# Late phase boundaries: the residual turned by plain transposes and scaled afterwards, with ScalarE's and VectorE's orders, and four one-column products for sixteen

## What is computed

```python
def second_block(...):
    for l in range(DEPTH):
        h = rmsnorm(x, norm_pre[l, 0]) * (1.0 + sc1) + sh1
        y = swiglu(h, ffn_w_gate[l, 0], ffn_w_up[l, 0], ffn_w_down[l, 0])
        x = x + 0.5 * g1 * rmsnorm(y, norm_post[l, 0])
        h = rmsnorm(x, norm_pre[l, 1]) * (1.0 + sc2) + sh2
        y = hybrid_mixer(h, ...)
        x = x + g2 * rmsnorm(y, norm_post[l, 1])
        ...
```

## Time and profile before

| | before |
|---|---|
| median of 3 runs | 3181.19 us (3179.10 to 3194.51) |
| the profiled execution | 3182.83 us |
| its span | 3181.0 us |
| mean granted clock of TensorE | 0.989 |
| busy: PE, DVE, ACT, POOL | 3090.9, 2255.9, 1637.7, 692.7 us |
| chain that ended last | PE 86%, DVE 8%, DMA 2%, ACT 2% |

### The profile page before, as it was taken

The page is one execution under the profiler, slowest core; times in us unless marked ns, Lnnn a source line. Parts: engine busy times, 40 slices in busy tenths (PEclk is TensorE's granted clock), DMA queues, the critical chain, the costliest instruction groups (busy, mean ns, idle before and its releaser), DMA issues.

```text
span 3181.0 us, 58397 instructions
## 1 busy us (share of the span) xinstructions
PE 3090.9 (97%) x19928; PEld 2753.1 (87%) x19928; DVE 2255.9 (71%) x4134; ACT 1637.7 (51%) x3094; POOL 692.7 (22%) x692
## 2 busy tenths in 40 slices
PE   6999999999999999999999999999999999999999
PEld 5779999988888876899999788879987998988898
DVE  6649988877777435798888677777666777766654
ACT  1225578864444354355888444455455545445543
POOL 0107845520000110285555000000100010010000
PEclk9999999999999998999999999999999999999999
DMA  7635555558887431455444788877854787884354
GB/s 284 240 134 167 187 165 173 163 204 264 262 259 253 130 120 40 136 184 170 139 138 133 251 263 262 261 248 260 264 197 141 248 262 257 276 260 144 123 183 152
DMA packets 178000, 635.86 MB, mean 200 GB/s; under 512 B 23976, under 2 KB 23984, under 8 KB 177232
## 3 DMA queue, kind: packets, MB, share of 16 engines
q1 hardware_dynamic: 134560, 491.48, 46.9%
q0 software_dynamic: 43296, 142.77, 13.5%
q10 hardware_dynamic: 16, 0.01, 0.0%
HBM read 630.88 MB, written 9.53 MB: 201 GB/s over the span
## 4 chain that ended last, share of the span: by engine, by line
PE 86%; DVE 8%; DMA 2%; DVEq 2%; ACT 2%; issue 1%; SPq 0%; ACTq 0%
PE ps L773 21%; PE ps L597 12%; PE ps L599 11%; PE ps L598 11%; PE ps L755 7%; PE ps L585 6%; PE ps L632 2%; PE ps L1167 2%; PE ps L1166 2%; PE ps L1035 1%; DMA ring<-stream 1%; PE ps L968 1%; PE ps L873 1%; PE ps L701 1%; PE ps L660 1%
## 5 line engine op out<-in xcount | busy, mean ns | idle before, releaser
L1781 DVE TENSOR_TENSOR unit_low<-ring,unit_high 128x1024 fp32r<-128x1024 f32 x480 | 638.8, 1331 | 172.3 <-ACT unit_high L1267 163.8
L1267 ACT CAST unit_high<-ring 128x1024 fp32r<-128x1024 f32 x524 | 548.2, 1047 | 230.6 <-PE ps L599 167.3
L599 PE MATMUL ps<-expert_x_high,unit_low 128*128 128x256 f32 x1968 | 556.1, 283 | 0.0
L597 PE MATMUL ps<-expert_x_high,unit_high 128*128 128x256 f32 x1552 | 447.9, 289 | 2.0 <-DVE unit_low L1781 1.8
L598 PE MATMUL ps<-expert_x_low,unit_high 128*128 128x256 f32 x1552 | 433.8, 280 | 0.0
L599 PEld LDWEIGHTS ps<-expert_x_high,unit_low 128*128 128x128 f32 x1968 | 370.5, 188 | 0.0
L773 PE MATMUL ps<-unit_low,expert_high 128*128 128x512 f32 x1016 | 325.1, 401 | 2.4 <-DVE unit_low L1781 2.4
L773 PE MATMUL ps<-unit_high,expert_high 128*128 128x512 f32 x1016 | 317.6, 393 | 4.6 <-ACT unit_high L1267 4.4
L773 PE MATMUL ps<-unit_high,expert_low 128*128 128x512 f32 x1016 | 320.1, 395 | 0.1
L597 PEld LDWEIGHTS ps<-expert_x_high,unit_high 128*128 128x128 f32 x1552 | 294.2, 190 | 6.5 <-issue 2.6
L598 PEld LDWEIGHTS ps<-expert_x_low,unit_high 128*128 128x128 f32 x1552 | 293.3, 189 | 0.0
(11 more groups left out here) (388 smaller groups left out, 7054.6 us busy)
## 6 DMA issues: line engine op xcount, KB each, us to landing
ring<-stream SPq DMA_DIRECT2D x754, 512.0 KB, 4.1
arena<-stream SPq DMA_DIRECT2D x160, 512.0 KB, 4.3
score<-ada POOLq DMA_DIRECT2D x128, 512.0 KB, 5.1
arena<-ada POOLq DMA_DIRECT2D x96, 512.0 KB, 5.1
arena<-bias_tiles POOLq DMA_DIRECT2D x48, 192.0 KB, 2.7
arena<-ada SPq DMA_DIRECT2D x8, 1024.0 KB, 17.3
bias_tiles<-bias_rows POOLq DMA_DIRECT2D x8, 768.0 KB, 14.9
arena<-gate_home POOLq DMA_DIRECT2D x7, 512.0 KB, 10.3
```

Source lines behind the costliest of these rows:

```text
L597: pe.matmul(out, hi[:, kt, :], xh[:, kt, :], start=(kt == 0), stop=False)
L599: mm = pe.matmul(out, lo[:, kt, :], xh[:, kt, :], start=False, stop=(kt == KD - 1))
L1267: nc.scalar.copy(hi, raw_of(unit)).then_inc(whi_ready, 1)
L1781: V.tensor_tensor(out=lo, in0=raw_of(unit), in1=hi, op=ALU.subtract).then_inc(wlo_ready, 1)
```

## The change

1. `turn_x` transposes x with the plain identity as its pieces arrive, so that it needs no root. After 6 dummies, two products spread the inverse roots of the two token halves over all partitions, into banks 3 and 2 (`row_scaled`).
2. DVE copies these rows to SBUF, multiplies each turned tile by its gain and by the row (`turned_in`), and ACT adds the shift (`shift`, as in the earlier phases). For a feed-forward phase DVE makes the low half from the unshifted tile in one instruction per tile.
3. ACT squares the first token half of x in one instruction of 1024 columns, after the last root of y. DVE does all four adds, then the inverses; the third unit's subtraction moves behind the adds, ahead of the second inverse.
4. In the hybrid POOL adds the squares of a group's four chunks, so that four one-column products do for sixteen; in round 3 DVE subtracts the unit `b + 3` ahead of the copies of the outputs.
5. Dummies: 14 for 12 at the hybrid's end, 6 for 8 at peer1's, none at the last phase's.

```diff
-            def turn_x(no, bank):
+            def turn_x(ph, bank):
+                i = PHASES.index(ph)
                 for tt in range(TT):
-                    pe.wait_ge(x_scaled, TT * no + tt + 1)
                     for kt in range(KD):
-                        mm = pe.matmul(hx(kt)[:, tt * P:(tt + 1) * P], xt[:, tt, kt * P:(kt + 1) * P], stat[:, tt, 0:P],
-                                       start=True, stop=True)
-                        if tt and kt % 2:
-                            mm.then_inc(hx_ready, 1)
-                    if tt == 0:
-                        busy(3, bank)
+                        if kt % 4 == 0:
+                            pe.wait_ge(x_ready, KD * (i - 1) + (4, 6, 6, 8)[2 * tt + kt // 4])
...
+                        pe.transpose(hx(kt)[:, tt * P:(tt + 1) * P], xt[:, tt, kt * P:(kt + 1) * P], ident)
+                busy(6, bank)
+                for tt in range(TT):
+                    pe.wait_ge(x_scaled, TT * (i - 4) + tt + 1)
+                    pe.matmul(ps[3 - tt][:, 0:P], x_inv[:, tt:tt + 1].to_broadcast([P, P]), ident,
+                              start=True, stop=True).then_inc(row_scaled, 1)
...
-                pe.wait_ge(osq_ready, KD * (l + 1))
+                pe.wait_ge(osq_added, 6 * (l + 1))
                 for grp in range(2):
                     for tt in range(TT):
-                        for kt in range(4):
-                            mm = pe.matmul(ps[3][:, 2 * grp + tt:2 * grp + tt + 1], sq[:, 4 * grp + kt, tt * P:(tt + 1) * P],
-                                           ones[:, 0:1], start=(kt == 0), stop=(kt == 3))
+                        mm = pe.matmul(ps[3][:, 2 * grp + tt:2 * grp + tt + 1], sq[:, 4 * grp, tt * P:(tt + 1) * P],
+                                       ones[:, 0:1], start=True, stop=True)
...
+            def x_first_half(ph):
+                act.wait_ge(x_ready, KD * PHASES.index(ph) + 4)
+                nc.scalar.activation(junk[:, 0:2, :], xt[:, 0, :].rearrange("p (q n) -> p q n", q=2), ACT.Square,
+                                     accum_out=x_sum[:, 0:1])
                 act.drain()
+                nc.scalar.activation(x_root[:, 0:1], x_sum[:, 0:1], ACT.Sqrt, bias=eps, scale=1.0 / D).then_inc(x_rooted, 1)
...
             def turned_in(ph):
                 vec = vec_of(ph)
-                for q in range(4):
-                    dve.wait_ge(h_ready, KD * norm_no_h[ph] + 2 * q + 2)
-                    for kt in (2 * q, 2 * q + 1):
-                        V.tensor_scalar(hT[:, kt, :], hx(kt), acol[:, kt:kt + 1], mods[:, vec, kt:kt + 1], ALU.mult, ALU.add)
-                    dve.drain()
-                    V.tensor_tensor(out=xparts[:, 1, 2 * q:2 * q + 2, :], in0=hT[:, 2 * q:2 * q + 2, :],
-                                    in1=xparts[:, 0, 2 * q:2 * q + 2, :], op=ALU.subtract).then_inc(xlo_ready, 2)
+                for tt in range(TT):
+                    dve.wait_ge(row_scaled, TT * (PHASES.index(ph) - 4) + tt + 1)
+                    V.tensor_copy(stat[:, 0, tt * P:(tt + 1) * P], ps[3 - tt][:, 0:P])
+                dve.drain()
+                for kt in range(KD):
+                    V.scalar_tensor_tensor(out=hT[:, kt, :], in0=hx(kt), scalar=acol[:, kt:kt + 1], in1=stat[:, 0, :],
+                                           op0=ALU.mult, op1=ALU.mult).then_inc(mid_ready, 1)
+                for kt in range(KD if ph.startswith("ffn") else 0):
+                    dve.wait_ge(h_ready, KD * norm_no_h[ph] + kt + 1)
+                    V.scalar_tensor_tensor(out=xparts[:, 1, kt, :], in0=hT[:, kt, :], scalar=mods[:, vec, kt:kt + 1],
+                                           in1=xparts[:, 0, kt, :], op0=ALU.add, op1=ALU.subtract).then_inc(xlo_ready, 1)
...
                 y_scale(1)
                 add(2)
+                add(3)
                 if more:
                     x_scaled_of(ph, 0)
-                add(3)
-                if more:
-                    x_halved_of(ph, 1)
+                    x_halved_of(ph)
+                    if nxt:
+                        low(start[nxt] + 2, split0[nxt] + 2)
                     x_scaled_of(ph, 1)
...
+                def add_squares(r):
+                    pool.wait_ge(osq_ready, KD * l + r + 1)
+                    first, chunk = 4 * (r % 2), r // 2 + 4 * (r % 2)
+                    pool.drain()
+                    G.tensor_tensor(out=sq[:, first, :], in0=sq[:, first, :], in1=sq[:, chunk, :], op=ALU.add).then_inc(osq_added, 1)
```

More of the change, by code:

```diff
@@ L1083, in hyb @@
                 pe.wait_ge(first_mixed, l + 1)
-                busy(12, ps[0])
+                busy(14, ps[0])
             def ffn(ph, no, u):
@@ L1216, in peer @@
                     pe.wait_ge(xt_ready, 1)
-                    busy(8)
+                    busy(6, ps[1])
                     return
@@ L1290, in shift @@
                     act.wait_ge(mid_ready, KD * n + kt + 1)
-                    nc.scalar.activation(hT[:, kt, :], hT[:, kt, :], ACT.Identity, bias=mods[:, vec, kt:kt + 1]).then_inc(h_ready, 1)
-            def turned_in(ph):
-                no = PHASES.index(ph) - 4
-                for kt in range(KD):
-                    act.wait_ge(hx_ready, 4 * no + kt // 2 + 1)
                     out = xparts[:, 0, kt, :] if ph.startswith("ffn") else hT[:, kt, :]
-                    nc.scalar.activation(out, hx(kt), ACT.Identity, bias=mods[:, vec_of(ph), kt:kt + 1],
-                                         scale=acol[:, kt:kt + 1]).then_inc(h_ready, 1)
-                if ph.startswith("ffn"):
-                    have(ACT.Silu)
+                    nc.scalar.activation(out, hT[:, kt, :], ACT.Identity, bias=mods[:, vec, kt:kt + 1]).then_inc(h_ready, 1)
             def x_square(ph, k):
@@ L1738, in peer @@
                     x_square(ph, 3)
[L1739 removed]
+                    x_second_half(ph)
                     return
@@ L1749, in _ @@
             for ph in phases:
-                if late_phase(ph):
-                    turned_in(ph)
-                else:
+                if not late_phase(ph):
                     norm_in(norm_no[ph], ph)
-                    if ph == "mix0":
-                        act.wait_ge(ada_read, 2)
-                    shift(ph, vec_of(ph))
+                if ph == "mix0":
+                    act.wait_ge(ada_read, 2)
+                shift(ph, vec_of(ph))
+                if ph.startswith("ffn"):
+                    have(ACT.Silu)
                 u = start[ph]
@@ L1871, in add @@
                     V.tensor_tensor(out=piece_of(xt, k), in0=piece_of(xt, k), in1=piece_of(yt, k), op=ALU.add).then_inc(x_ready, 2)
-                for k in range(3):
+                for k in range(4):
                     gated(k)
                     add(k)
-                x_halved_of(ph, 0)
-                gated(3)
                 x_scaled_of(ph, 0)
-                add(3)
-                x_halved_of(ph, 1)
+                x_halved_of(ph)
+                low(start[nxt] + 2, split0[nxt] + 2)
                 x_scaled_of(ph, 1)
-                low(start[nxt] + 2, split0[nxt] + 2)
             def add_normed(ph):
@@ L1949, in add_normed @@
                     gate(0)
-                    if nxt:
-                        low(start[nxt] + 2, split0[nxt] + 2)
                     gate(1)
@@ L2286, in hyb @@
                         project(qs[:, 0], ps[1], b3[:, i + 1, :], -SCALE)
+                    if i == 3:
+                        low(b + 3, m + 3)
                     take_outputs(r, i)
@@ L2291, in hyb @@
                         lowest(g, k, causal[k])
-                    low(b + 4 if i < 3 else b + 3, m + 3)
+                    if i < 3:
+                        low(b + 4, m + 3)
                     for k in range(2):
@@ L2686, in hyb @@
                             bias(e, f, i + (16 + 4 * f) if e == 0 else i * 2 + (24 + f))
+                    for r in (2 * i - 2, 2 * i - 1) if i >= 2 else ():
+                        add_squares(r)
+                add_squares(6)
+                add_squares(7)
             def row_out(ph, col):
```

40 lines of the change are left out of this document (18 added, 22 removed).

## The result

| | before | after |
|---|---|---|
| median, first comparison | 3180.14 us (4 runs) | 3158.71 us (4 runs, 3155.66 to 3166.69) |
| ratio | | 0.9923, 95% interval 0.9897 to 0.9948 |
| median, later runs | 3180.25 to 3185.48 us | 3161.75 us (12 runs), 0.9933 (0.9911 to 0.9955) |
| profiled execution, its span | 3182.83, 3181.0 us | 3166.69, 3164.9 us |
| chain that ended last | PE 86%, DVE 8% | PE 90%, DVE 4% |

What follows compares the result with a forecast made beforehand. PE, busy for 97% of the span, was taken as the bound. Hybrids 11.7 plus handoffs 5.5 gave 17.2 us: 3182.8 to 3165.6 us for a profiled execution, 3164 us for the median, range 3154 to 3175.

Steps and rivals of the forecast that it cites:

- one-column products: Tail of both hybrids on PE: going from 16 products to 4 saves 2.6 and about 2.8 us, 5.4 us.
- half clock behind them: PE behind the hybrids' one-column products: the half clock is their consequence and goes with them, 4.4 us, lower bound 0.
- hybrid's subtraction: Hybrid, round 3: moving DVE's subtraction ahead of the outputs' copies removes PE's 0.95 us wait in both hybrids, 1.9 us.
- chains of the long handoffs: hyb0 to ffn1, ffn1 to ffn2, hyb1 to ffn3: shorter chains to the first product save 3.8, 2.5 and 2.2 us.
- clock given back there: Three long handoffs: PE's remaining pauses still cost half clock, 1.0 us at each, between 0 and 1.7.
- short handoffs: The three short handoffs: removed scaled turns balance added dummies, row products, copy and scaling, 0.0 within 0.3 us at each.
- low halves in the ffns: Low halves made on DVE for the ffns are ready before PE wants each: 0.
- rival D: The clock stays up throughout; nothing is given back: 20 to 25 us saved, 3160 to 3157 us; chance 0.15.
- Rival B: Half clock at all six handoffs grows into two stretches each, 3.4 us lost per handoff: 3183 us; chance 0.03.
- Rival A: Transposes do not hold the clock; each of six handoffs gets a half-clock stretch of 1.7 us: 3171 us; chance 0.20.
- Rival C: Hybrid's tail: ACT's casts and DVE's subtractions hold PE; some 3 of the 11.7 us come: 3173 us; chance 0.10.
- POOL's additions: Hybrid: six additions of 256 columns on POOL, 0.6 us each, at most 2.4, hidden at cost 0.

Runs made afterwards that it cites:

- experiment 2: Changed kernel with the hybrid's round-3 subtraction back behind DVE's minima, ahead of the normalisation, as before the change: 3161.2 us, ratio 0.9943.
- experiment 5: Changed kernel without the six dummies between the transposes of x and the two row products, at all six handoffs: 3159.2 us, ratio 0.9932.
- experiment 8: Changed kernel with six dummies moved behind the row products: 3156.4 us, repeated 3156.7; then also 19 dummies instead of 14 behind each hybrid: 3155.9 us, repeated 3158.5.
- experiment 3: Changed kernel with the third unit's subtraction for the next ffn early again, between mixes or gates instead of behind the last adds: 3168.9 us, ratio 0.9966.
- experiments 6 and 7: Changed kernel with every last-third dummy replaced by two plain transposes: 3163.8 us; changed kernel without any last-third dummy: 3164.2 us.
- experiment 1: Changed kernel with the hybrid's sixteen one-column products back in place of four, without POOL's additions: 3171.4 us, ratio 0.9981.
- the changed kernel again: The changed kernel, unaltered, in a second set of runs with its own profile: 3161.8 us over 12 runs, ratio 0.9933.
- the kernel with ordinary products: Changed kernel with x turned by ordinary products against the identity (32 records a handoff) instead of 16 transposes: 3167.8 us, ratio 0.9949.

## Why the prediction was right, and where it was not

3164 us was forecast, 3154 to 3175 as the range; 3158.7 and 3161.8 were measured. The sum was 17.2 us, the last third shows 20.6. The waits and their order were right, and the clock at the handoffs was not. Part of the closeness is luck: two terms put at nothing came to -1.2 and 2.0 us and nearly cancel, and the profiled execution (3166.7 against 3165.6 forecast for it) lost 4.5 us ahead of the last third, which hid the surplus.

| step | forecast | measured | by |
|---|---|---|---|
| one-column products | 5.4 | 5.4 | 2.68 in each hybrid |
| half clock behind them | 4.4 | 4.3 | hybrids' 11.1 less the other two |
| hybrid's subtraction | 1.9 | 1.4 | experiment 2 |
| chains of the long handoffs | 8.5 | 8.7 | 3.88 + 2.77 + 2.03 |
| clock given back there | -3.0 | 0 | 1.00 in all windows |
| short handoffs | 0 | -1.2 | 0.52 + 0.30 + 0.37 longer |
| low halves in the ffns | 0 | 2.0 | ffn lengths |

- **The long chain was right in its steps.** Last reciprocal at 2457.18 (2457.3 to 2457.5 forecast), row products at 2457.95 (2457.9), copies of 0.26 us (0.29), DVE's scaling to PE's first product 1.17 us (1.17), first product at 2460.13 (2460.2). The scalings run at 0.40 us each out of PSUM, so no 0.5 us came on top.
- **"I give back 1.0 us at each of the three" failed.** Both pauses are there at hyb0 to ffn1 as forecast, 1.61 and 1.57 us (the first is 0.78 at ffn1 to ffn2 and 1.96 at hyb1 to ffn3), and the clock stays at 1.00. The step took it that such pauses cost a stretch. They do not by themselves: with the six dummies taken out between them (experiment 5) two of the three long handoffs still cost none. The third then has one behind it, so the dummies may have kept it there; experiment 8's stretch is not explained by them, and experiment 3 has one after shorter pauses than two others without. That the clock held is shown, in both profiles; what decides it is open. It is rival D's case, for the handoffs.
- **"The three short ones: 0.0" failed** by the dummies. They hold the row products back by 1.2 us there (experiment 8: 6.72 and 6.66 us with the dummies behind, against 7.94 and 7.95), where the long ones lose 0.7.
- **"The low halves are ready before each is: 0"** was true of the kernel after and overlooked the kernel before, where PE waited for the last pair of them. The ffns are 0.4 to 0.7 us shorter each, 0.4 to 0.5 of it by this wait.
- **The moved subtraction's 1.9** was mis-sized; it measured 1.4: behind the wait stood another.
- **Rival B misread a row.** The 3.79 us of the earlier trace rows are 16 records but eight turns, half of the turning; its price does not rest on that.
- **Rival A** fell: no handoff has a stretch, and experiments 6 and 7 show that the transposes hold the clock. Rival B falls with the same windows. **Rival C** fell: the output rows run at full clock with PE's one new wait of 0.34 us.
- **POOL's additions** took 0.72 to 1.79 us, where I had 0.6 and at most 2.4; hidden as forecast, with 1.9 us to spare.

## What to carry to other kernels

Put filler work for the clock where the engine waits anyway and nothing is queued behind it that others wait for: the same six dummies cost 0.7 to 1.2 us a handoff ahead of the row products and nothing behind them. Do not judge a pause by its length alone: look at the granted clock of each place, in more than one profile. Where an engine turns data in the chain, count its records: 16 records fewer were 1.8 us a handoff here. When the clock makes medians scatter by more than a change is worth, compare the changed part between two marks in the profiles; behind the first handoff it repeated to 0.2 us.

## What the hardware showed that I had not expected

- **One-column products.** 32 records, busy without a gap for 3.5 us, are followed by 3.4 to 6.6 us at half clock; 8 records in 0.95 us are not (experiment 1). PE is busy for the whole of both, so the busy share gives no warning. Why the one is followed by half clock and the other is not, no run here shows.
- **Transposes of fp32 tiles held the clock at these handoffs as well as products did** (experiments 6 and 7).
- **The same pause costs a stretch in one profile and none in another**: 1.96 us at hyb1 to ffn3, with the same PE work up to it (experiment 8 and the changed kernel).
- **POOL's addition of 256 columns** takes 0.73 to 0.79 us, but 1.67 and 1.79 us when it starts within 0.13 us behind a 1024-column subtraction on DVE:

```profile
2427.51 1.22 DVE L1777 TENSOR_TENSOR unit_low<-ring,unit_high 128x1024 fp32r<-128x1024 f32 x1
...
2431.50 1.22 DVE L1777 TENSOR_TENSOR unit_low<-ring,unit_high 128x1024 fp32r<-128x1024 f32 x1
```

  DVE's own 1.22 us are what it takes elsewhere. In experiment 2, where the first of these subtractions stands later, it is the other way round in hyb0: the addition starts 0.23 us ahead of it and takes 0.91 us, and the subtraction takes 1.76. The Trainium skill (GPSIMD Engine Reference, 8. Key points) says that GpSimd shares its SBUF interfaces with VectorE and that instructions of VectorE with two SBUF inputs contend with it; these rows agree with it, by about 1 us an addition.
- **A cast on DVE can wait for POOL for 16 us.** DVE's cast of 128x256 integers to fp32 in the peer phases takes 0.29 us when POOL starts its next instruction behind it. When POOL has a subtraction in work, it ends 0.15 us after that one does, after 2.3 to 2.5 us. This holds in all fourteen profiles. In the three that reach peer1's end last (the changed kernel again, the first with the dummies behind, all transposes), POOL went on from the subtraction to a MEMSET, and the cast waited for both. Changed again, DVE, then POOL:

```profile
1458.22 16.18 DVE L2439 CAST pick<-r_ab 128x256 f32<-128x256 uint32 x1
...
1458.16 2.40 POOL L2613 TENSOR_TENSOR unit_low<-ring,unit_high_early 128x1024 fp32r<-128x1024 f32 x1 [0.31 <-ACT unit_high_early L1272]
1460.50 13.76 POOL L2708 MEMSET arena<- 128x16384 f32 x1
```

  The two starts lie 0.06 us apart, so I take which case a run gets for a matter of small shifts. Both kernels have this place; taking it out was not tried.
- **Open.** What decides whether a pause at a handoff costs a stretch, why the half-clock stretches ahead of 2131 us differ so much from run to run, and why the kernel with ordinary products, alone of all, stayed within 3.4 us over eight runs, was not followed up.
